# After each of three layer norms, one weight tile's products for both token blocks issued at once

## The reference

```python
h = x
for i in range(DEPTH):                      # DEPTH = 2
    y = diff_attention(h, ...) if i % 2 == 0 else gla(h, ...)
    h = layer_norm(DN_ALPHA * h + y, ln_g[i, 0], ln_b[i, 0])
    f = squared_relu_mlp(h, mlp_w1[i], mlp_w2[i])   # square(relu(h @ w1)) @ w2
    h = layer_norm(DN_ALPHA * h + f, ln_g[i, 1], ln_b[i, 1])
```

## Time and profile before

| what | value |
|---|---|
| median of 3 runs | 2107.2 us |
| profiled execution, its own time | 2107.15 us |
| its span | 2105.4 us |
| PE busy | 2099.0 us, 100% of the span, 10916 matmuls |
| DVE busy | 1755.0 us, 83% |
| ACT busy | 1195.4 us, 57% |
| POOL busy | 189.0 us, 9% |
| granted clock of PE | 1.00 |

### The profile page before, as it was taken

How to read it: one execution, slowest core, us unless ns; L and a number is a source line. 1 busy time by engine, 2 the same in 40 slices (tenths; PEclk the granted TensorE clock), 3 DMA queues, 4 the chain that set the end, 5 groups by cost and what they waited for, 6 DMA issues and landing times.

```text
span 2105.4 us, 27042 instructions
## 1 busy us (share of the span) xinstructions
PE 2099.0 (100%) x10916; PEld 1803.5 (86%) x10916; DVE 1755.0 (83%) x1495; ACT 1195.4 (57%) x1067; POOL 189.0 (9%) x155
## 2 busy tenths in 40 slices
PE   9999999999999999999999999999999999999999
PEld 8888888988888888888898888889888888888887
DVE  5555549978988988989788888797989989989888
ACT  5443445456656655666455566445655666666563
POOL 3000000300000000000030021102000000000000
PEclk9999999999999999999999999999999999999999
DMA  9445546579889889888846778776789889898884
GB/s 326 164 143 200 174 161 219 192 230 279 245 231 286 248 250 264 261 234 239 292 140 198 218 223 246 256 224 219 208 253 260 257 237 261 247 276 244 231 246 179
DMA packets 241761, 487.37 MB, mean 231 GB/s; under 512 B 7856, under 2 KB 7856, under 8 KB 240624
## 3 DMA queue, kind: packets, MB, share of 16 engines
q1 hardware_dynamic: 204928, 406.61, 54.6%
q0 software_dynamic: 36288, 78.39, 20.5%
q10 hardware_dynamic: 432, 0.79, 0.1%
HBM read 483.66 MB, written 2.10 MB: 231 GB/s over the span
## 4 chain that ended last, share of the span: by engine, by line
PE 99%; DVE 0%; DMA 0%; ACT 0%; issue 0%; ACTq 0%
PE ps L686 59%; PE ps L1030 9%; PE ps L1028 8%; PE ps L1034 8%; PE ps L908 2%; PE ps L963 1%; PE ps L965 1%; PE ps L970 1%; PE ps L1233 1%; PE ps L1227 1%; PE ps L1229 1%; PE ps L1249 1%; PE ps L1247 1%; PE ps L1254 1%; PE ps L1268 1%; PE ps L761 1%
## 5 line engine op out<-in xcount | busy, mean ns | idle before, releaser
L686 PE MATMUL ps<-X,hi 128*128 128x512 f32 (+1 forms) x3008 | 697.0, 377 | 0.1
L686 PEld LDWEIGHTS ps<-X,hi 128*128 128x128 f32 x3008 | 549.2, 188 | 99.7 <-issue 0.2
L1555 ACT ACTIVATE hi<-raw 128x2048 fp32r<-128x2048 f32 x196 | 372.6, 1915 | 230.4 <-DVE raw L2243 149.0
L2229 DVE TENSOR_TENSOR lo<-raw,hi 128x2048 fp32r<-128x2048 f32 x196 | 444.7, 2286 | 20.1 <-PE ps L1034 10.8
L686 PE MATMUL ps<-X,lo 128*128 128x256 f32 x2816 | 387.0, 283 | 0.0
L686 PEld LDWEIGHTS ps<-X,lo 128*128 128x128 f32 x2816 | 373.2, 191 | 12.8
L1833 DVE TENSOR_TENSOR lo<-raw,hi 128x2048 fp32r<-128x2048 f32 x104 | 237.6, 2296 | 106.1 <-ACT hi L1336 99.9
L1336 ACT ACTIVATE hi<-raw 128x2048 fp32r<-128x2048 f32 x118 | 224.3, 1914 | 156.2 <-PE ps L686 114.9
L2229 DVE TENSOR_TENSOR lo<-up_raw,hi 128x2048 fp32r<-128x2048 f32 x112 | 256.0, 2286 | 31.7 <-PE ps L686 31.7
L1539 ACT ACTIVATE hi<-up_raw 128x2048 fp32r<-128x2048 f32 x112 | 214.3, 1913 | 27.2 <-PE ps L1034 11.4
L1030 PE MATMUL ps<-hi,forms 128*128 128x512 f32 x448 | 175.5, 392 | 0.0
(11 more groups left out here) (284 smaller groups left out, 2814.1 us busy)
## 6 DMA issues: line engine op xcount, KB each, us to landing
raw<-in_mlp_w_dram SPq DMA_DIRECT2D x144, 1024.0 KB, 7.7
up_raw<-in_mlp_w_dram SPq DMA_DIRECT2D x112, 1024.0 KB, 7.8
raw<-in_mlp_w_dram POOLq DMA_DIRECT2D x56, 1024.0 KB, 9.5
raw<-in_gla_w_in_dram SPq DMA_DIRECT2D x48, 1024.0 KB, 5.6
raw<-in_attn_w_qkv_dram SPq DMA_DIRECT2D x47, 1024.0 KB, 5.2
raw<-in_attn_w_o_dram SPq DMA_DIRECT2D x16, 1024.0 KB, 5.5
raw<-in_gla_w_o_dram SPq DMA_DIRECT2D x16, 1024.0 KB, 6.8
raw<-in_gla_w_in_dram POOLq DMA_DIRECT2D x8, 1024.0 KB, 9.4
```

The source lines that it names most:

```text
L686: return pe.matmul(o, w, m, start=start, stop=stop)
L1555: act.activation(hi[:, P_AT[p] % 4], raw[:, slot], ACT.Copy).then_inc(hi_ready, 2 if p == PRODUCTS - 1 else 1)
L2229: dve.tensor_tensor(lo[:, at % 3], src, hi[:, at % 4].bitcast(F32), ALU.subtract).then_inc(lo_ready, n)
```

## The change

`cols_by_block` leaves the last tile (j = 3) out of the first pass. In the second pass that tile's matmuls with high weights take all 256 tokens at once, both parts: 16 matmuls of 512 columns in the place of 16 of 256 columns in either pass. Its matmuls with low weights stay. Three of the four transposes in the table move, since the places they stood at are gone or lie at other times: quarter 5 from (0, 3, 0) to (1, 0, 0), quarter 6 from (1, 0, 1) to (1, 0, 3), quarter 7 from (1, 1, 1) to (1, 1, 2). The last tile waits for both `hi_ready` and `lo_ready` in the second pass. Nothing is changed in the order of DVE, ACT, POOL or SP.

```diff
             def cols_by_block(g, L, after=None):
-                turn = {(0, 2, 0): 4, (0, 3, 0): 5, (1, 0, 1): 6, (1, 1, 1): 7}
+                turn = {(0, 2, 0): 4, (1, 0, 0): 5, (1, 0, 3): 6, (1, 1, 2): 7}
+                last = TILES - 1
                 for t in range(TB):
-                    for j in range(TILES):
-                        if t == 0:
+                    for j in range(TILES if t else last):
+                        if t == 0 or j == last:
                             pe.wait_ge(hi_ready, 4 * g + j + 1)
-                        else:
+                        if t:
                             pe.wait_ge(lo_ready, 4 * g + j + 1)
                         pe.wait_ge(x_lo, 8 * L + QUARTERS * t + j + 1)
                         for k in range(KPT):
                             a = 4 * j + k
                             for i in range(4):
-                                acc = ps[:, i, :].rearrange("p (s t) -> p s t", s=2)
-                                m = mm(acc[:, :, blk(t)], hi[:, j, k, blk(i)], X[:, a, :, blk(t)], t == 0 and a == 0, False)
+                                if j == last:
+                                    mm(ps[:, i, :], hi[:, j, k, blk(i)], X[:, a, :, :], False, False)
+                                else:
+                                    acc = ps[:, i, :].rearrange("p (s t) -> p s t", s=2)
+                                    m = mm(acc[:, :, blk(t)], hi[:, j, k, blk(i)], X[:, a, :, blk(t)], t == 0 and a == 0, False)
                                 if t:
-                                    m = mm(acc[:, 0, :], lo[:, j, k, blk(i)], X[:, a, 0, :], False, a == KT - 1)
+                                    m = mm(ps[:, i, 0:SEQ], lo[:, j, k, blk(i)], X[:, a, 0, :], False, a == KT - 1)
```

## The result

The changed kernel takes 2113.91 us, the median of 8 runs (2113.49 to 2114.05), against 2107.19 us before: 6.7 us more, ratio 1.0031 with a 95% interval of 1.0022 to 1.0040. The forecast was 2113.2 us, with a range of 2110.7 to 2114.6. The profiled execution took 2113.49 us of its own; it was the fastest of the eight.

What follows compares the result with a forecast made beforehand. The prediction took PE, busy 2099.0 of 2105.4 us, to bound the kernel. Added waits less saved matmuls gave 2.0 + 2.1 + 2.0 = 6.1 us over three calls, on 2107.15: 2113.2 us, range 2110.7 to 2114.6.

Steps and rivals of the forecast that it cites:

- 1. first matmul of the second pass: First call: PE waits 0.89 us for the low part of X quarter 4, restarts in 0.12, starts at 396.96.
- 2. X low 5 starts: First call, DVE: idle 0.64 us for ACT's copy of quarter 5, start at 399.21; everything queued behind moves by 0.64.
- 4. weight low 2 ends: First call, DVE: ends at 406.95; PE at tile 2 waits 0.22 us and restarts in 0.12.
- 5. next group: First call's end on PE: the next group starts at 416.54 in place of 414.52, 2.02 us more.
- The saving: In each call, 32 matmuls of 256 columns become 16 of 512: 0.19 us less, 0.58 over three calls.
- step 3: First call, tile 1: weight low 1, taking 2.53 us, ends at 402.34; PE waits 0.74 us and restarts in 0.12.
- my extra 0.1: GLA call: quarter 4's low part starts 6.52 us behind the pass's start against 6.41, so 2.1 us.
- The bound from below: Without the 0.64 us DVE delay and all restarts: 1.26 us a call, 3.8 in all, 2110.9 us.
- Rival A: At the second pass's start the cover holds and only the 0.58 us saving shows: 2106.6 us; chance 0.03.
- Rival B: In the calls PE waits, but DVE is not thrown back by 0.64 us: 2110.9 us; chance 0.15.
- Rival C: DVE thrown back further, weight low 2 0.25 us longer beside POOL's scaling: 2114 to 2114.7 us; chance 0.10.
- Rival D: Last tile: alternating wide and narrow matmuls cost over 0.348 us a pair; 0.03 more gives 2114.6 us; chance 0.04.

Runs made afterwards that it cites:

- experiment 3: Changed kernel with the last tile's 16 matmuls of 512 columns made as 32 of 256 again, still all in the second pass: 2112.99 us.
- experiment 1: Kernel before with only the new places of the transposes of X quarters 5, 6 and 7, no tile wide: 2110.58 us.
- experiment 2: Changed kernel with quarter 5's transposes at the end of the first pass, (0, 2, 3), in place of (1, 0, 0): 2112.31 us.
- experiment 5: Changed kernel with high weights first in tiles 1 to 3 and, on DVE, X low 4 ahead of scale 1: 2108.36 us.
- again: The changed kernel, unaltered, run a second time beside the other variants on one chip: 2113.71 us.

## Why the prediction was right, and where it was not

The sign, the places and the order of the waits came as forecast, and so did the median, within 0.7 us. The mechanism was right; two sizes in it and one term beside it were not. In the first call, with the 0.11 us of the later start taken off:

| step | forecast | measured |
|---|---|---|
| 1. first matmul of the second pass | 396.96 | 396.91 |
| 2. quarter 5's transposes | 397.92 | 397.94 |
| 2. X low 5 starts | 399.21 | 399.21 |
| 3. weight low 1 ends | 402.34 | 402.10 |
| 4. weight low 2 ends | 406.95 | 406.70 |
| 5. last tile begins | 410.97 | 410.70 |
| 5. next group | 416.54 | 416.35 |

- **The saving** of 48 matmuls came (48 fewer), but a pair of a wide and a narrow one costs 0.353 us, 5.65 over 16, where I had 0.348. Merging saves 0.11 us a call (experiment 3) and not 0.19.
- **The term that was too large** is the length of weight low 1 in step 3. I moved today's 2.53 us along with it; moved, it took 2.28 like the others. That is the 0.25 us by which the rest of the call came sooner, and with the dearer pairs the call cost 1.83 and not 2.02. So PE lost 0.46 us at tile 1 where the forecast has 0.86 (a wait of 0.74 and the restart). What makes it 2.53 or 2.28 was not tried. It took 2.46, 2.53 and 2.49 us in experiments 1, 2 and 5, and POOL's scaling that began beside it took 2.62 us before (400.41 to 403.03) and 3.02 with the change (400.51 to 403.53), so POOL lost 0.40 us where DVE gained 0.25. In experiments 2 and 5, with DVE's at 2.53 and 2.49, POOL's took 2.62 again.
- **The GLA call** cost 1.84 us, no more than the others; my extra 0.1 was wrong, the gate's products behind cost nothing, as said.
- **The bound from below** held: 1.26 us a call, and experiment 2, which takes the DVE delay away, has 1.4.
- **The term that was missing** is the 0.8 to 1.3 us outside the calls, for the most part in the GLA heads. I looked for where instructions stand and wait, and not at what a shorter program does to its own fetching. It brought the median up to 2113.91 where the calls alone make 2112.7. The two errors, 0.6 us too much in the calls and 1.3 left out beside them, have opposite signs, so the closeness of 2113.2 is in part luck.
- **Rival A** fell with the first row of waits. **Rival B** is experiment 2: it needed the transposes of quarter 5 in another place. **Rival C** had the sign wrong: the weight low parts did not get longer. **Rival D** was right in kind with 0.005 us a pair.

## What to carry to other kernels

Where PE never waits, look at what it would wait for next: two engines 1.5 us apart can both look free of waits, and work taken from PE ahead of that point is only worth what is in hand. A transpose that feeds another engine is placed by that engine's clock, and its lateness is paid at the product behind it. And if two variants differ in the median where their stretches agree, compare the other stretches before giving the difference to the edit: the length of the program alone moved this one by 0.8 us.

## What the runs showed of the hardware that I had not expected

- 190 instructions that do nothing useful, each behind a matmul of 0.228 us, cost PE nothing where they stand (the groups that hold them take the same time within 0.02 us) and the kernel 0.85 us by the medians. With them 0.02 MB of program is fetched 7 to 8 us into a 1 MB load, which lands after 10.4 us in place of 9.3.
- A wait with the releaser "issue" (0.56 and 0.33 us) reads as a wait for DVE: again, the data's end lay 0.07 us ahead of the weight load's start, and in all eight traces the product starts 0.10 or 0.11 us behind that end.
- The same DVE subtraction of 128x2048 took 2.53 us at 399.17 before and 2.28 at 399.93 after, with the same work on DVE around it.
